# Prompt blocks' scores and values moved into the page bundles of a hybrid attention kernel

## The reference

```python
q, k, v, g_a, u, v_s, g_b, m_a, m_b = split(rmsnorm(x) @ w_in)      # 1024 -> 5632
# prompt: 8 heads of 64, query blocks of 128, keys of the own and the earlier blocks
s = (q * scale) @ k.T + relative_bias;  p = softmax(causal(s));  attn = p @ v
# samples: the same over the pages, of which each query keeps the 3 blocks of 256 best by q . mean(k)
y_a = attn * silu(g_a);  y_b = spatial(u, layernorm(v_s)) * silu(g_b)
out = rmsnorm(x + (sig(m_a) * (y_a @ w_pa) + sig(m_b) * (y_b @ w_pb)) @ w_o)
```

## Time and profile before

| | |
|---|---|
| median of 3 runs | 540.87 us (538.53 to 541.87) |
| profiled execution, its own time | 539.03 us |
| its span | 537.2 us |
| mean granted clock of the tensor engine | 0.989 |
| tensor engine (PE) busy | 518.3 us (96%) |
| vector engine (DVE) busy | 315.4 us (59%) |
| scalar engine (ACT) busy | 178.1 us (33%) |
| GpSimd (POOL) busy | 120.3 us (22%) |
| DMA | 112.00 MB, mean 208 GB/s |

### The profile page before, as it was taken

One profiled execution on the slowest core, in us unless ns is written; L12 is line 12 of the kernel. 1 busy time (PEld: TensorE's weight loads), 2 busy tenths in 40 slices (PEclk: granted clock), 3 DMA queues, 4 the chain that ended last, 5 costly groups with the idle time before them and its releaser, 6 DMA issues.

```text
span 537.2 us, 13838 instructions
## 1 busy us (share of the span) xinstructions
PE 518.3 (96%) x5624; PEld 473.1 (88%) x5624; DVE 315.4 (59%) x686; ACT 178.1 (33%) x389; POOL 120.3 (22%) x108
## 2 busy tenths in 40 slices
PE   8999999979999999999998898999999999999993
PEld 6999999968889988998998898998999999998672
DVE  6624333477864865766853678986662553793524
ACT  5532222124332432433532342131152232342314
POOL 1201111211321322211321325542245100000002
PEclk9999999989999999999999899999999999999998
DMA  8745633287467888877598978868859993360004
GB/s 238 206 157 143 214 122 121 63 273 222 153 214 224 289 255 267 277 210 250 171 309 265 337 252 272 282 219 287 280 183 302 316 337 96 128 235 1 2 10 156
DMA packets 73561, 112.00 MB, mean 208 GB/s; under 512 B 5501, under 2 KB 35338, under 8 KB 73498
## 3 DMA queue, kind: packets, MB, share of 16 engines
q1 hardware_dynamic: 72122, 107.51, 62.0%
q0 software_dynamic: 1232, 3.36, 2.1%
q10 hardware_dynamic: 144, 0.26, 0.1%
HBM read 106.57 MB, written 4.53 MB: 207 GB/s over the span
## 4 chain that ended last, share of the span: by engine, by line
PE 78%; DVE 6%; SPq 6%; DMA 4%; issue 3%; ACT 2%; POOL 1%; POOLq 0%; DVEq 0%; ACTq 0%
PE BK L625 37%; PE BK L645 9%; PE BK L967 8%; PE BK L796 4%; PE BK L782 4%; DMA KRAW<-in_cache_k 4%; SPq L551 2%; PE BK L714 2%; PE BK L844 2%; PE BK L659 2%; PE BK L861 2%; PE BK L851 1%; DVE KT L1375 1%; DVE NMX L1479 1%; SPq L531 1%
## 5 line engine op out<-in xcount | busy, mean ns | idle before, releaser
L625 PE MATMUL BK<-XH,WH 128*128 128x272 f32 x672 | 203.2, 302 | 6.1 <-ACT G L1016 3.2
L625 PE MATMUL BK<-XH,WL 128*128 128x272 f32 x672 | 194.7, 290 | 0.0
L625 PE MATMUL BK<-XL,WH 128*128 128x272 f32 x672 | 194.2, 289 | 0.0
L625 PEld LDWEIGHTS BK<-XH,WH 128*128 128x128 f32 x672 | 127.5, 190 | 17.7 <-issue 10.8
L625 PEld LDWEIGHTS BK<-XL,WH 128*128 128x128 f32 x672 | 127.6, 190 | 0.0
L625 PEld LDWEIGHTS BK<-XH,WL 128*128 128x128 f32 x672 | 127.1, 189 | 0.0
L1375 DVE STREAM_TRANSPOSE KT<-KRAW 128x512 f32<-128x512 f32 x128 | 86.6, 696 | 58.0 <-DMA KRAW<-in_cache_k 53.7
L1737 POOL TENSOR_TENSOR WL<-WRAW,WH 128x1024 fp32r<-128x1024 f32 x32 | 76.7, 2396 | 191.9 <-ACT WH L1016 191.9
L1016 ACT ACTIVATE WH<-WRAW 128x1024 fp32r<-128x1024 f32 x52 | 55.0, 1057 | 15.6 <-PE BK L645 15.6
L1266 DVE TENSOR_TENSOR WL<-WRAW,WH 128x1024 fp32r<-128x1024 f32 x19 | 23.3, 1224 | 37.2 <-ACT WH L1016 37.1
L782 PE MATMUL BK<-KT,QW 128*32 128x128 f32 x1024 | 35.5, 280 | 0.0
(11 more groups left out here) (207 smaller groups left out, 803.8 us busy)
## 6 DMA issues: line engine op xcount, KB each, us to landing
KRAW<-in_cache_k SPq DMA_DIRECT2D x128, 256.0 KB, 4.3
WRAW<-in_w_in SPq DMA_DIRECT2D x21, 1024.0 KB, 7.1
VRAW<-in_cache_v SPq DMA_DIRECT2D x56, 256.0 KB, 4.0
VQT<-in_cache_v SPq DMA_DIRECT2D x28, 256.0 KB, 3.6
VEX<-in_cache_v SPq DMA_DIRECT2D x24, 256.0 KB, 4.1
VGU<-in_cache_v SPq DMA_DIRECT2D x20, 256.0 KB, 3.5
WO<-in_w_o SPq DMA_DIRECT2D x4, 1024.0 KB, 6.6
XR<-in_x_prompt SPq DMA_DIRECT2D x4, 512.0 KB, 5.5
```

The costliest lines, as they stand in the source:

```text
L625: last = mm(BK[h][:, 0:HALF], w[:, n % 2, k, :], x[:, k, cols], start=(i == 0 and w is WH and x is XA), stop=(i == KC - 1 and w is WL))
```

## The change

The prompt blocks' scores move to the steps 4, 8, 12 of each 16, so that they stand behind the page bundle in the same step, and their values, four steps on, do too (8, 12, 16). Values come ahead of the next block's scores. The turn moves from the middle of step s+3 to its beginning, ahead of the fill. Values are written to the score bank of the sample whose turn is next; scores wait for the scalar engine's copy (a0_ok) instead of the gate (av_ev), and page scores of a new sample wait for the gates of the blocks whose values lay in its bank. The vector and scalar engines' loops use `block_at` too, so their parts of a block move with it.

```diff
 def block_at(t):
-    if t % 16 in (5, 10, 15) and 5 <= t < 16 * PAIRS:
-        return 3 * (t // 16) + t % 16 // 5 - 1
+    if t % 16 in (4, 8, 12) and 4 <= t < 16 * PAIRS:
+        return 3 * (t // 16) + t % 16 // 4 - 1
     return None
+
+def block_bank(i):
+    return (i // 3 + 1) % 2
...
# page_scores
                     wait(pe, pt_ok, b - 1)
+                    wait(pe, av_ev, min(3 * b, len(BLOCKS)))
...
# prompt_scores
-                wait(pe, av_ev, i)
+                wait(pe, a0_ok, 2 * i)
...
# prompt_values
                 pe.wait_ge(a0_ok, 2 * i + 2)
+                wait(pe, av_ev, i)
+                wait(pe, pt_ok, i // 3)
...
-                            last = mm(BK[6][hd, x * P:(x + 1) * P], VROW[...],
+                            last = mm(SCB[block_bank(i)][hd, x * P:(x + 1) * P], VROW[...],
...
# the tensor engine's loop
             for t in range(STEPS):
+                if block_at(t - 3) is not None:
+                    prompt_turn(block_at(t - 3))
                 run(fill, 2 if t % 2 == 0 or t >= PAGES else 1 if t < 64 else 3)
...
-                if block_at(t - 3) is not None:
-                    prompt_turn(block_at(t - 3))
                 if block_at(t - 4) is not None:
                     prompt_values(block_at(t - 4))
                 if block_at(t) is not None:
                     prompt_scores(block_at(t))
...
# prompt_gate
-                dve.tensor_tensor(g, BK[6][:, 0:len(ys) * P], g, ALU.mult).then_inc(av_ev, 1)
+                dve.tensor_tensor(g, SCB[block_bank(i)][:, 0:len(ys) * P], g, ALU.mult).then_inc(av_ev, 1)
```

More of the change, by code:

```diff
@@ L860, in prompt_values @@
                             hd = slice(e * HD, (e + 1) * HD)
-                            last = mm(BK[6][hd, x * P:(x + 1) * P], VROW[:, j, c * P + e * HD:c * P + (e + 1) * HD],
+                            last = mm(SCB[block_bank(i)][hd, x * P:(x + 1) * P], VROW[:, j, c * P + e * HD:c * P + (e + 1) * HD],
                                       APT[:, e, o + j * P:o + (j + 1) * P], start=(j == 0), stop=(j == y))
```

## The result

The changed kernel took 562.00 us (median of 4 runs, 561.38 to 562.75) against 540.67 us (4 runs, 538.53 to 541.87) for the kernel before on the same chip: a ratio of 1.0394, with an interval of 1.0368 to 1.042. It is 21.3 us, 3.9%, slower. The forecast was 555 and its range 546 to 567: the right side and the right mechanism, but 7 us short.

A forecast was written before the change was run, and what follows sets the result against it. The tensor engine was taken as the bound. Waits +22.9, old waits -0.7, merging -4.8, turns +0.9 and first block -2.8 gave +15.5 on 539.03 us: 554.5, stated as 555 us, range 546 to 567.

The forecast's parts named there:

- Waits before the turns: Tensor engine idle ahead of all twelve prompt turns until the vector engine's scaling ends; 22.9 us in total.
- middle blocks: Second block of each column: turn reached 4.35 us after scores start, relay needs 6.45; wait 2.1 us each.
- last blocks: Last block of each column: turn reached 4.55 us after scores start, relay needs 6.2; wait 1.65 us each.
- first blocks: First block of a column: turn reached 4.80 us after scores start, relay 6.54 as measured; wait 1.8 us each.
- The old waits: Tensor engine's two waits for the scaling before the change, expected to go; -0.7 us.
- The very first block: Around the split-weights wait: scores cost nothing there (-1.1 us), clock loss gone (-1.7), but its turn waits 2.5.
- The clock: Rival: longer gaps before turns also lower the clock, about 1.6 us each, +8 to +19, 563 to 574; chance 0.17.
- Merging: 24 prompt score and value pieces joining page bundles lose their own stops, 0.20 us each; -4.8 us.
- Bank, semaphores, queues: Values in the next sample's score bank, scores waiting for the copy, the load queue's and POOL's waits; 0 us.
- Transfers as the bound: Rival: page and weight arrivals pace the stretch from 265 us, absorbing the delay; 538 or 535 us; chance 0.05.
- turns alone: Turns moved in front of their step all stand alone; 8 of them pay a first fill; +0.9 us.
- first scores in the gap: First block's scores stand ahead of the 2.85 us wait for split weights and cost nothing; 1.1 us gained.

The follow-up runs named there:

- the changed kernel with the split held back: Changed kernel with POOL's split due in step 19 waiting until the first sample's choice on the vector engine is done; 560.46 us, ratio 1.0365.
- the extra stops in page bundles: Kernel before, with one unit of fill moved between page scores and page values in the 16 page bundles of steps 64 to 124; 543.93 us.
- the kernel with the old step numbers: Changed kernel with scores at steps 5, 10, 15 and the turn in the middle of step s+3, leaving the new bank and semaphores; 539.60 us.
- the first attempt at the vector engine's order: Changed kernel with first page sums moved from step 9 to 11 below step 64 and all gates from s+5 to s+7; 566.29 us.
- the second version of the later gates: Changed kernel with page sums at step 11 and only the first two blocks' gates of each column behind the scaling; 558.10 us.
- the fastest kernel: Changed kernel with the turn ahead of step s+4's page scores and POOL's step-19 split waiting for the first sample's choice; 535.42 us.

## Why the prediction was right in kind and short by 7 us

The sum gave +15.5 us on the profiled execution; it came out at +22.4. Term by term:

- **Waits before the turns: right.** 22.9 predicted. The gaps add up to 20.1 in the trace; measured as the distance of starts beyond the fill's cadence they are 22.0. By kind: middle blocks 2.09, 1.82, 1.94 and 1.82 (2.1 predicted), last blocks 2.20, 1.55, 1.72 and 1.73 (1.65), first blocks 2.14, 1.77 and 2.21 (1.8). Block 7's scaling ended at 6.24 us, against 6.40 by the sum; block 6's at 6.53, against 6.54. Blocks 3 and 9 were later than that (8.75 and 6.96) because the choice held the vector engine when their scores came, and in both one small instruction of the choice was stretched beside POOL's split (2.45 us at 150.97, 1.99 us at 240.78). The old waits' 0.7 to 0.9 went, as said.
- **The very first block: two errors that cancel.** I took its clock loss as gone behind a shorter wait and put its turn's wait at 2.5. The wait for the split weights was 1.96 us and the clock still fell to 0.53 behind it (111.0 to 114.6 us). Fill at half clock reached the turn later, so that the turn waited only 0.98. The half clock ran under the wait.
- **The clock: the step that failed.** I had it as a rival with a chance of 0.17, in which the longer gaps lose the clock. Behind blocks 1, 2 and 9 the granted clock fell to 0.5, and with it fill matmuls came every 0.23 us instead of 0.125. Each fall costs 1.3 to 1.6 us: 4.4 together. I had weighed the place between the gap that kept the clock and the one that lost it by "none so short has done it here". That no row held a gap between 1.50 and 2.85 us was no evidence on either side (the trace before holds one more stop, 2.71 us at 296.8, and it lost the clock too), and the sum put five of the twelve waits at 2.1 or more. How many falls come is in part luck: the changed kernel with the split held back makes the same stop before block 9, 2.06 us against 2.05, keeps the clock, and has its next page scores 1.55 us sooner.
- **The silu wait: not in the sum.** +1.9. Before, L1435 began 2.2 us ahead of POOL's split (144.12, 146.31); the change moved it 6.9 us later and the split 4.7, and the two met.
- **Merging: 4.1 instead of 4.8.** The piece at 221 us shows each part. Page values take the 0.99 that they took before, and prompt values 0.81 up to the scores' start, as they took 0.81 up to the fill's; only the 0.10 on entry and the 0.10 of the first fill are saved, 0.20 each, as taken. But the passage from a page's small pieces (L837, L830) to the prompt values costs 0.07 to 0.18 that it did not cost before. The Trainium skill (TensorEngine Tiling (Array Packing), Key Properties) says that a change of tiling mode drains the engine; the trace agrees, with 0.09 to 0.11 a change that merging didn't save, and the extra stops in page bundles, which add a change of mode, with 0.31 to 0.35 instead of 0.20.
- **Bank, semaphores, queues: 0, right**, by the kernel with the old step numbers. It holds only for this place of the gate, as the first attempt at the vector engine's order showed.
- **Transfers as the bound: wrong, as said.** The stretch from step 68 to 128 starts 22.6 us late and ends 22.4 late.

Waits 22.0, old waits -0.9, merging -4.1, turns alone +0.8, first scores in the gap -1.1, three more falls of the clock +4.4, silu +1.9: 23.0, against 23.1 between steps 4 and 68 and 22.4 in the spans. The clock's 4.4 and the silu's 1.9 make up the miss.

The remedy does not lie in the merging. What it earns by itself is 538.2 against 541.0, 2.8 us; the price came with the turn, which was put three steps behind the scores with little between but fill.

One thing stays open in part: why blocks 1 and 7 kept their waits when the vector engine's order was changed. The traces show POOL's split over the stretched scaling in both, and none over that of blocks 4 and 10; but moving the split away from the scaling was not tried.

## What to carry to other kernels

When pieces are merged to save stops, count for each relay across engines what lay between its ends, and keep the last end as late as the work that needs it allows: here 24 merged pieces earn 4 us and twelve turns that came 1.0 to 2.2 us too early, three to six units of fill, cost 20. A wait moved to an idle place is free only at that place; moving its releaser by two steps made it 9.5 us. When a sum holds waits near the longest one that is known to keep the clock, put the falls into the sum, as a range.

## What the runs showed of the hardware that was not expected

- **Clock.** In the stops that these traces hold between 100 and 460 us, none of up to 1.81 us was followed by a fall of the granted clock. Of the longer ones some were and some were not, and the length alone does not tell which: the clock fell behind 1.85 us (the second version of the later gates, at 112.8 us), 1.92, 1.96, 2.05 and 2.05 (the kernel after) and 2.85; it stayed behind 1.98 in the kernel after, 2.01 in the fastest kernel, 2.04 in the second version and even 3.22 in the first version of the later gates. The windows right behind the 2.01 us, behind the 3.22 us, and behind the 2.06 us before block 9 in the changed kernel with the split held back, to be held against the 0.50 at 252.2 us above:

```profile
110.90:114.50 3.60, 3.23 (x24) 3.00 (x24) 3.53 (x12) 0.69 (x4) 0.00 (x0) 1.00 0.87 273
```

```profile
247.70:252.70 5.00, 5.00 (x96) 4.47 (x97) 2.36 (x9) 0.92 (x4) 0.00 (x0) 1.00 0.59 171
```

```profile
251.10:254.30 3.20, 3.20 (x45) 3.05 (x49) 1.13 (x2) 1.35 (x3) 2.40 (x1) 1.00 0.83 286
```

- **Vector engine beside POOL.** An instruction of 0.17 to 0.23 us took 1.97 to 2.45 us when it met POOL's split of 2.4 us: a product of two tables (L1445) and a comparison of 8 columns (L1447), and each ended within 0.1 us of the split's end. The first scaling instruction of 384 columns took 1.29 us instead of 0.38 in the same way, while page transposes in the same microseconds kept their 0.7 us. The kernel before has it too: an addition of 32 columns (L1438, 0.19 us elsewhere) took 2.31 us at 307.37, beside a split from 307.26 us on.
- **A stop of the tensor engine** costs 0.20 us between pieces of different tile shapes, and 0.31 to 0.35 between two of one shape.
